# First expert layer: gated in place, context first, every third dot split between GpSimd and ScalarE

## The reference, cut to what matters

```python
def peer(h, w_q, sub_keys, u, v):          # h: (512, 1024); u, v: (16384, 1024)
    q = (h @ w_q).reshape(T, 8, 2, 128)
    s = einsum('thpd,hpnd->thpn', q, sub_keys)        # 8 heads x 2 sides x 128 keys
    sv, si = top_k(s, 16)
    cand = (sv[:, :, 0, :, None] + sv[:, :, 1, None, :]).reshape(T, 8, 256)
    fv, fi = top_k(cand, 16)
    idx = i1 * 128 + i2                               # 128 experts of each token
    g = softmax(fv)
    act = gelu(einsum('td,ted->te', h, u[idx]))
    return einsum('te,ted->td', g * act, v[idx])
```

## Time and profile before

| what | value |
|---|---|
| median of 3 runs | 3766.13 us (3762.77 to 3767.57) |
| profiled execution, its own time | 3757.47 us |
| its span | 3755.7 us |
| PE busy | 3287.2 us (88%) |
| DVE busy | 2497.0 us (66%) |
| ACT busy | 874.4 us (23%) |
| POOL busy | 883.1 us (24%) |
| DMA, mean | 262 GB/s |
| the stage `both_experts` in the span | 1475.8 to 2796.0 us |

### The profile page before, as it was taken

How to read it: one execution, slowest core, us unless ns; L and a number is a source line. 1 busy time by engine, 2 the same in 40 slices (tenths; PEclk the granted TensorE clock), 3 DMA queues, 4 the chain that set the end, 5 groups by cost and what they waited for, 6 DMA issues and landing times. The chain is left out here.

```text
span 3755.7 us, 56484 instructions
## 1 busy us (share of the span) xinstructions
PE 3287.2 (88%) x22342; PEld 2862.1 (76%) x22359; DVE 2497.0 (66%) x4759; ACT 874.4 (23%) x1601; POOL 883.1 (24%) x804
## 2 busy tenths in 40 slices
PE   9998999998999978999499987778879897599876
PEld 9976999986997657887388866666657687488875
DVE  5556656555664364589988857767775488877745
ACT  4345434334443353111022200000014411110000
POOL 0000000000000001014555545555530033423432
PEclk9999999999999999999799999999999999899998
DMA  7652666642662204279899999999971289999998
GB/s 245 224 176 101 234 222 205 230 160 90 230 211 84 73 1 152 73 234 394 306 355 369 363 364 403 400 403 404 404 290 49 97 336 409 349 361 342 406 409 316
DMA packets 298406, 983.68 MB, mean 262 GB/s; under 512 B 32928, under 2 KB 66720, under 8 KB 297248
## 3 DMA queue, kind: packets, MB, share of 16 engines
q1 hardware_dynamic: 187552, 577.36, 43.6%
q0 software_dynamic: 110592, 402.70, 27.6%
HBM read 960.01 MB, written 19.92 MB: 261 GB/s over the span
## 5 line engine op out<-in xcount | busy, mean ns | idle before, releaser
L325 PE MATMUL banks<-h_whole,ring 128*128 128x256 f32 (+1 forms) x4352 | 782.6, 336 | 138.0 <-ACT acts_out L2459 54.0
L325 PEld LDWEIGHTS banks<-h_whole,ring 128*128 128x128 f32 x4352 | 677.1, 193 | 214.4 <-ACT big L2914 84.7
L300 DVE TENSOR_TENSOR ring_lo<-ring,ring_hi 128x1024 fp32r<-128x1024 f32 x365 | 448.0, 1228 | 370.4 <-ACT ring_hi L294 351.1
L325 PE MATMUL banks<-scratch,ring 128*128 128x256 f32 x2048 | 490.1, 396 | 126.6 <-DVE scratch L2269 126.3
L325 PEld LDWEIGHTS banks<-scratch,ring 128*128 128x128 f32 x2048 | 392.8, 196 | 224.0 <-DVE scratch L2269 171.2
L294 ACT ACTIVATE ring_hi<-ring 128x1024 fp32r<-128x1024 f32 x365 | 386.7, 1059 | 571.1 <-PE banks L315 512.2
L325 PE MATMUL banks<-big,ring 128*128 128x128 f32 x2048 | 260.8, 281 | 50.7 <-DMA ring<-peer_v_dram 47.8
L311 PE MATMUL banks<-h_parts,ring_hi 128*128 128x256 f32 x1160 | 287.2, 286 | 6.0 <-PEq L664 3.4
L325 PEld LDWEIGHTS banks<-big,ring 128*128 128x128 f32 x2048 | 238.0, 192 | 70.2 <-DMA ring<-peer_v_dram 66.8
L312 PE MATMUL banks<-h_parts,ring_hi 128*128 128x256 f32 x1160 | 283.8, 282 | 0.0
L311 PEld LDWEIGHTS banks<-h_parts,ring_hi 128*128 128x128 f32 x1160 | 221.7, 191 | 18.3 <-issue 17.8
(11 more groups left out here) (366 smaller groups left out, 5852.5 us busy)
## 6 DMA issues: line engine op xcount, KB each, us to landing
ring<-peer_u_dram SPq DMA_DIRECT2D x256, 512.0 KB
ring<-peer_v_dram SPq DMA_DIRECT2D x256, 512.0 KB
big<-mod_w_dram SPq DMA_DIRECT2D x96, 512.0 KB, 4.6
ring<-ffn_gate_dram SPq DMA_DIRECT2D x88, 512.0 KB
ring<-ffn_up_dram SPq DMA_DIRECT2D x88, 512.0 KB
ring<-ffn_down_dram SPq DMA_DIRECT2D x88, 512.0 KB
ring<-peer_q_dram SPq DMA_DIRECT2D x32, 512.0 KB
act_store<-acts_out SPq DMA_DIRECT2D x128, 128.0 KB
```

The lines of the kernel that those rows point to most:

```text
L300: self.nc.vector.tensor_tensor(self.lo[:, self.slot(j)], self.ring[:, self.slot(j)], self.hi[:, n % 2].bitcast(F32), ALU.subtract).then_in ...
L325: ins = self.nc.tensor.matmul(out, self.ring[:, self.slot(j), c * P:(c + 1) * P], b, start=opens and m == 0, stop=opens and m == len(terms ...
```

## The change

- The stage before (`out_by_stream`) makes the ctx output first and norms it, so that `both_experts` begins with ctx tokens ready and norms x itself. Queries run as 32 tiles (16 for ctx, then the same 16 fetched again for x).
- Ctx is chosen first and by head pairs: for each pair of heads and token half a `level` (top 16 of four rows of 128) and a `choices` for two heads; 32 gathers become possible after each.
- Gelu writes into `A`, which stays in SBUF; `act_store`, its stores and loads, and the copy to `G` are gone. Gates are made for half of the keys at a time (128 steps, half of them woven into `fall`), and VectorE multiplies them from PSUM into `A`.
- Of the 256 dots every third (85) is taken from VectorE: GpSimd multiplies the row buffer by the tokens, in the POOL queue between the gathers, and ScalarE sums it with a copy that accumulates. ScalarE's place for each sum is planned from an estimated clock.
- Six row buffers instead of five; `spend` lets in a token step for every 2000 columns.
- The transposes of the choices stand behind `rise(95)` instead of `rise(57)`.

```diff
-ROWS = 5
+ROWS = 6
@@ both_experts
-    bufs = (whole_x[:, 0:D], whole_x[:, D:2 * D], whole_ctx[:, 0:D], whole_ctx[:, D:2 * D], spare[:, 0])
+    bufs = (whole_ctx[:, 0:D], whole_ctx[:, D:2 * D], k.rows[:, 0], whole_x[:, 0:D], whole_x[:, D:2 * D],
+            k.acts[:].rearrange("p r t -> p (r t)"))
+    LEAD = 4
+    order = [(0, t, 32 * b + p) for b in range(B) for t in range(NT) for p in range(32)] + [(1, 0, p) for p in range(LEAD)]
+    order += [(1, t, p + LEAD * (1 - t)) for p in range(P - LEAD) for t in (1, 0)] + [(1, 1, p) for p in range(P - LEAD, P)]
+    apart = [n for n in range(NT * P) if n % 3 == 2]
+    own_steps = [n for n in range(len(order)) if n not in apart]
+    EXP_X, SELECTED, FIRST_GATES = 93, 95, 96
+    steps_before, expected, QUERY, TILE = {}, {}, 3460, 3460
+    gates_after = [[n for n in range(STEPS) if FIRST_GATES + n * (N - 1 - FIRST_GATES) // STEPS == e] for e in range(N)]
+    gates_under = [[n for n in range(STEPS, 2 * STEPS) if (n - STEPS) * (HALF - 8) // STEPS == r] for r in range(N)]
...
-                sp.wait_ge(acted.sem, acted.after(e + 1))
-                sp.dma_start(k.act_store[e], k.acts[:, e % R]).then_inc(k.act_stored[e % R].sem, 16)
...
-                act_load(e, e - R + 1)
...
         @block.gpsimd
+            def multiply(n):
+                t = order[n][1]
+                pool.wait_ge(k.row_loaded[n % ROWS].sem, k.row_loaded[n % ROWS].after(16 * (n // ROWS + 1)))
+                nc.gpsimd.tensor_tensor(bufs[n % ROWS], bufs[n % ROWS], tok[:, t], ALU.mult).then_inc(multiplied.sem, 1)
+            for n, (table, t, p) in enumerate(order):
+                if not table and p % 32 == 0:
+                    pool.wait_ge(ready.sem, ready.after(n // 32 + 1))
+                before = n - ROWS
+                if before >= 0:
+                    freed = apart_used if before in apart else used
+                    pool.wait_ge(freed.sem, freed.after(nth[before] + 1))
                 nc.gpsimd.indirect_dma_start(bufs[n % ROWS], None, rows_of[table], ...)
+                if n - 2 in apart:
+                    multiply(n - 2)
@@ vector
-                    if spent >= 1150:
-                        spent -= 1150
+                    if spent >= 2000 and own_steps[step] < 32 * units:
+                        spent -= 2000
                         token_step()
+            for b in range(B):
+                for t in range(NT):
+                    level(1, t, b)
+                    LEVELS[1], steps_before["levels", 1] = count, step
+                    SETTLED[1] = choices(1, t, 2 * b, 2)
...
+            for n in range(2 * STEPS + 1):
+                if n < 2 * STEPS:
+                    mark(n)
+                if n:
+                    weigh(n - 1)
+                for _ in range(n % 2 if n < STEPS else 1 + (n % 3 == 0)):
+                    if n >= STEPS or step < OWN_DOTS:
+                        token_step()
+            while step < len(own_steps):
+                token_step()
@@ scalar
+            def apart_sums(last):
+                while summed_apart < len(apart) and apart[summed_apart] <= last:
+                    n = apart[summed_apart]
+                    summed_apart += 1
+                    act.wait_ge(multiplied.sem, multiplied.after(summed_apart))
+                    nc.scalar.activation(bufs[n % ROWS], bufs[n % ROWS], ACT.Copy,
+                                         accum_out=act_of[:, order[n][1], order[n][2]:order[n][2] + 1]).then_inc(apart_used.sem, 1)
+            def keep_up(now, coming):
+                ready_by = [n for n in apart if expected.get(n - 1, now) + 2000 < now]
+                within = own_steps[max(0, min([steps_before[w] for w in coming] + [len(own_steps)]) - 1)]
+                apart_sums(min(max(ready_by, default=0), within))
-                nc.scalar.activation(k.acts[:, e % R], k.ps[:, 4 + e % 2, 0:T], ACT.Gelu).then_inc(acted.sem, 1)
+                nc.scalar.activation(A[:, e], k.ps[:, 4 + e % 2, 0:T], ACT.Gelu).then_inc(acted.sem, 1)
```

More of the change, by code:

```diff
@@ L2197, in choices @@
+                pairings += 1
+                spend(wide)
+                made(nc.vector.tensor_copy(sif[m][:, rows], si[m][:, rows]), 32 * many)
+                dve.wait_ge(pairs.sem, pairs.after(pairings))
+                sixteen(range(many), cand, cand_left, fv[:, heads], fi[:, heads], lambda n: None)
                 dve.wait_ge(top.sem, top.after(count))
                 flat = fi[:, heads].rearrange("p a b -> p (a b)")
-                made(nc.vector.tensor_scalar(part[:, 0, cols], flat, 4, None, ALU.logical_shift_right), 128)
@@ L2216, in choices @@
-                if m == 1:
-                    dve.wait_ge(after.sem, after.after(n))
-                    nc.vector.scalar_tensor_tensor(idx[:, t], chosen[:, 0, cols], float(NKEYS), chosen[:, 1, cols], ALU.mult,
-                                                   ALU.add).then_inc(ready.sem, 1)
-                units += 1
-                return n
+                whole = made(nc.vector.tensor_copy(partf[:, :, cols], part[:, :, cols]), 32 * many)
+                picks = [pick[w][:, 0:16 * many] for w in range(2)]
@@ new lines, in choices @@
+                for w in range(2):
+                    dve.wait_ge(after.sem, after.after(at[w]))
+                    at[w] = made(nc.vector.reduce_sum(chosen[:, w, cols], picks[w], AX), wide)
+                if m == 1:
+                    dve.wait_ge(after.sem, after.after(at[1]))
+                    nc.vector.scalar_tensor_tensor(idx[:, t, 16 * first:16 * (first + many)], chosen[:, 0, cols], float(NKEYS),
+                                                   chosen[:, 1, cols], ALU.mult, ALU.add).then_inc(ready.sem, 1)
@@ L2378, in gates @@
                 last.then_inc(product.sem, 1)
             def fall(r):
-                pe.wait_ge(weighted.sem, weighted.after(r + 1))
-                k.whole(pe, Q + N + r, [(sums[:, c], c, hidden[:, r % R]) for c in range(KD)], False).then_inc(done.sem, 1)
+                k.whole(pe, V + r, [(sums[:, c], c, A[:, r]) for c in range(KD)], False).then_inc(done.sem, 1)
             for j in range(2):
-                query(j, 0)
+                query(j)
             sum_of_squares()
-            for j in range(2, R):
-                query(j, 0)
+            query(2)
@@ L2415, in _ @@
+                for n in gates_after[e]:
+                    gates(n)
             pe.wait_ge(kept.sem, kept.after(STEPS))
+            pe.wait_ge(acted.sem, acted.after(N))
             k.open_banks(range(4))
             for r in range(N - 1):
+                if r == HALF:
+                    pe.wait_ge(kept.sem, kept.after(2 * STEPS))
                 fall(r)
-            pe.wait_ge(weighted.sem, weighted.after(N))
+                for n in gates_under[r]:
+                    gates(n)
             for m in range(KD // 2):
-                k.whole(pe, Q + 2 * N - 1, [(sums[:, c], c, hidden[:, (N - 1) % R]) for c in (2 * m, 2 * m + 1)], False,
+                k.whole(pe, V + N - 1, [(sums[:, c], c, A[:, N - 1]) for c in (2 * m, 2 * m + 1)], False,
@@ L2950, in split_experts @@
     rstd_ends(k)
-    for b in range(ROWS):
-        k.row_loaded[b].ends(16 * len(range(b, len(order), ROWS)))
+    for b in range(W):
+        k.row_loaded[b].ends(16 * len(range(b, len(order), W)))
     tables.ends(16)
```

468 lines of the change are left out of this document (237 added, 231 removed).

## The result

The changed kernel takes 3993.14 us (median of 4 runs, 3987.88 to 3994.13); the kernel before took 3764.45 beside it (4 runs, 3754.14 to 3767.57). The ratio is 1.0614, 95% interval 1.0595 to 1.0633: 229 us slower. The forecast was 3739, its range 3665 to 3815.

The account below looks back on a forecast made before the run. The limit changes by stretch: TensorE, VectorE, both, then DMA at the end. Choosing to 2027, then 24, 173, 227, 310 and 8 us end the stage at 2769, 27 earlier: 3766 - 27 = 3739 us, range 3665 to 3815.

Parts of the forecast that it names:

- the overlap of TensorE's tiles with the choosing: In the choosing: TensorE reaches `rise(93)` by 1893 us, so its wait lies inside the choosing's end at 2027.
- First gather 1516, first dot 1522: Start of the choosing: first gather goes at about 1516 us instead of 1660.6, first dot at 1522.
- A round of 8.15 us: POOL queue in the choosing: product 2.5, issue 1.2, landing 4.1 and gaps 0.35 make 8.15 us per three gathers.
- The choosing ends at 2027: Choosing: 62 rounds of 8.15 us from 1522 end at 2027 us, against 1865.3 in the kernel before.
- First half of the gates 173: First gates after the choosing: VectorE's 142 us of steps and dots plus 31 us of blocking by GpSimd products.
- Second half 227: Gates under `fall`: VectorE 207 us and TensorE 205 us, with 10% added for mutual waits, give 227 us.
- The rest 310: End of the stage: 242 remaining pieces of gathers and tiles at 1.28 us each, DMA-bound, 310 us.
- The lock lengthens each round: Slower rival: dots hold the issue behind each product, round 9.05 us, 56 us on top, 3795 us; chance 0.30.
- The short chain: Faster rival: product 2.2, issue 0.94, landing 3.8, round 7.0 us, 71 us less, 3668 us; chance 0.16.
- Nothing: Rival: rounds of 8.5 to 8.7 us, earlier start and longer choosing cancel, 3759 to 3774 us; chance 0.12.
- The transfers were hidden anyway: Rival: the stage's end is not DMA-bound, so the 82 us of removed transfers are worth nothing; no separate chance given.
- VectorE's 2.4 us of spare time: In each round of the choosing VectorE has 2.4 us spare, nearly a whole product, so blocking is charged nothing there.

Follow-up runs that it names:

- e1_plan: Changed kernel without the cap on ScalarE's sums by later waits and without the demand for sums ahead of each move of scores: 3800.05 us.
- e2_cap: Changed kernel with only the cap on ScalarE's sums lifted, the demand ahead of x's scores kept: 3918.0 us.
- e9_due: Changed kernel with only the demand for sums ahead of x's scores removed, the sums still held behind later waits: 3889.81 us.
- e3_lag3: e1_plan with GpSimd multiplying each row three gathers after its issue instead of two: 3749.86 us.
- e6_sparse: e4_all_vector with a token step let in for every 2000 columns instead of 1350: 3733.64 us.
- e8_weave: e4_all_vector with two accumulating steps instead of one at another third of the 64 gate steps under `fall`: 3623.81 us.
- e12_beside: e7_five plus 85 extra GpSimd products of 1024 columns, one behind every third gather, into a buffer nothing reads: 3826.19 us.
- e4_all_vector: Changed kernel with all 256 dots on VectorE, none on GpSimd and ScalarE, a token step per 1350 columns: 3643.2 us.
- e7_five: e4_all_vector with five row buffers instead of six: 3656.59 us.
- e5_double: e3_lag3 with a second product in place behind each GpSimd product, waiting for it: 3983.63 us.

## Why the prediction was wrong

**The step that failed** is the overlap of TensorE's tiles with the choosing: "ScalarE follows a plan with a round of about 6.7 us, so at 8.15 it waits for products before its gelus, and TensorE follows it [...] so this wait is inside the 2027." The working took TensorE's tiles as free to stand at `rise(93)` by 1893 and let only the rounds set the end of the choosing. What the prediction read as a plan of times is an order. Sums up to row 98 stand in front of x's last queries, so tiles began at 1779 instead of 1605; and no later sum stands in front of gelu 70. Waits in both directions then follow one upon the other: rounds, with TensorE idle, then tiles, with the rounds stopped. Where the prediction has this wait inside the 2027, the trace has a hole of 235.8 us in the gathers and the last choice at 2240. Taking both conditions out brings 3993 to 3800 (e1_plan), and each alone leaves a hole (e2_cap, e9_due).

**Point by point.**
- First gather 1516, first dot 1522: 1510.2 and 1515.4. Right, and worth what was said.
- Product 2.5 us: 2.35. The Trainium skill's 2048-column figure in the GPSIMD Engine Reference, section 3.1, halved to 2.25 as an estimate, is nearer to this trace; the difference changes nothing.
- A round of 8.15 us: the 34th product starts at 1777.1 and the first at 1518.9, 258.2 / 33 = 7.82; from 2027.6 to the end of the choosing it is 8.2. The chain of row, product and issue is right, and e3_lag3 shows the landing in it.
- The choosing ends at 2027: 2240.2. That is 213 of the 257 us by which the stage ends later than forecast (3025.7 against 2769): 236 of the hole, less 7 for the earlier first dot and 16 for the rounds outside the hole.
- Choosing to gates 24: 21.7 (2240.2 to 2261.9). First half of the gates 173: 184 (2261.9 to 2446.1). Second half 227: 238 (to 2684). Terms of the right kind, 11 us short each.
- The rest 310: 335 (to 3019.3). The size of a piece was off. While TensorE's tiles and the gathers both fetch, the part runs near 400 GB/s as said, but TensorE is done early and waits 80.7 us for the last accumulating steps, and gathers alone need about 1.5 us each instead of 1.28. The order between tiles and gathers was missing from the sum.
- Outside the stage zero: 959.7 us behind it before and 960.4 after. Right.
- A tile of `rise`, 3.1: 3.45, the spacing of the gelus in the hole and in the trace of before too. By it `rise(93)` would have stood at 1926 instead of 1893, still inside the 2027.

The misses added up: 213 - 2 + 11 + 11 + 25 - 2 = 256.

**The rivals.** *The lock lengthens each round* was given 9.05 us, 3795 and a chance of 0.30. In the changed kernel the rounds stay below its bound of 8.7 (7.82 and 8.2). Its issues behind a product take a median of 0.98 us before the hole, but 1.78 after it, the 2.1 of the rival nearly. With the plan mended 44 of 61 take about 1.8, rounds are 8.75, and the kernel takes 3800. So the mechanism that the first rival named is real. It isn't the whole of the longer round: the issues have a mean of 1.57 us there, where the sum had 1.2, and from an issue's end to the next product it is 4.69, where the sum had 4.1 and gaps of 0.35. Why rows were used later was not followed up. The longer round puts the end of the choosing at 2057, 30 us after the forecast's 2027. The forecast of 3739 would have missed that kernel by 61 us, though its range would have held it. That the rival's 3795 is near 3800 is in part luck: its rounds of 9.05 are longer than measured, and the other 31 us come from behind the choosing. *The short chain* is out in all runs: the shortest rounds, 7.45 us with the product three behind (the 62 products of the choosing start from 1524.5 to 1979.0), are GpSimd's own work. *Nothing* did not come. *The transfers were hidden anyway* can't be read from these runs alone: no run puts the stores back. That the end is bound by what is left to fetch is shown by e6_sparse and e8_weave, which move pieces and pay or gain 1.5 and 0.9 us for each.

**Where the prediction charged nothing.** It let VectorE's 2.4 us of spare time in a round absorb each product. In a round that GpSimd paces that is nearly right. But it means that the edit had nothing to gain: a dot costs VectorE 1.14 us, and a product beside it 1.91 where VectorE is full (e12_beside), for a product of 1.90; the real one takes 2.35. From e4_all_vector to e3_lag3, 62 dots less and 62 products more should add 62 x (2.35 - 1.14) = 75 us to the choosing; it grows by 56 (1926.4 to 1982.3), with some hidden. Of the 107 us between the two runs 35 lie in the gates: the marks start from 1937.6 to 2343.0 in one and from 2000.3 to 2440.9 in the other. Where the last 16 lie was not followed up. The Trainium skill, SBUF — State Buffer, "SBUF: two separate sides", calls the shared ports of the two engines an exclusive lock. The traces agree for the dots: 1.91 us lost for 1.90 us of product. The estimate worked out from it in the prediction, that VectorE's round could grow to 8.2, was the better reason against the change.

What the change had right is visible once this part is out: the choosing by head pairs with the earlier gathers, activations gated in place and six buffers give 115 us, and 20 more with a better weave. The sixth buffer is 13 us of it (e7_five); how much each of the first two gives by itself was not tried, nor how much the later place of the transposes.

## What to carry to other kernels

An engine's program is an order, and a planned place is a wait with a due date: for each instruction put behind a condition, find what stands behind it on the same engine, and in a chain of three engines follow this once around. Before work is moved from VectorE to GpSimd, compare what GpSimd takes with what VectorE saves: elementwise work on one stopped elementwise work on the other here, so 2.35 us of product didn't pay for 1.14 us of dot. When a part is bound by what is left to fetch, count the pieces by kind, since those left alone at the end ran slower than a mixture.

## What the runs showed of the hardware

- A GpSimd product of 1024 columns took 2.35 us in place with two different inputs, and 1.90 with the same input twice and another output (which of the two counts was not tried). It took 3.22 where a held dot ran first (e5_double), and the issue of a gather took 1.78 instead of 0.94 to 0.98 in the same place (e1_plan).
- Beside a GpSimd product even a small VectorE operation can wait: a product of 128x32 elements took 2.33 us in the changed kernel, else 0.18. A dot could be held for the whole product:

```profile
1570.88 3.78 DVE L2139 CUSTOM_DVE_ANT_0 x_t<-x_t,h_whole 128x1024 f32<-128x1024 f32 x1
```

```profile
1571.22 2.35 POOL L2108 TENSOR_TENSOR acts_out<-acts_out,h_whole 128x1024 f32<-128x1024 f32 x1
```

- VectorE's searches, with one input, did not wait. In the changed kernel, inside the product that runs from 1518.95 to 1521.29, an index search takes the same 0.28 us as elsewhere, and the dot behind it is held:

```profile
1520.15 0.28 DVE L2185 FIND_INDEX8 big<-big 128x8 uint32<-128x128 f32 x1
1520.35 2.01 DVE L2139 CUSTOM_DVE_ANT_0 x_t<-x_t,h_whole 128x1024 f32<-128x1024 f32 x1
```

- A tile of `rise` takes 3.45 us (the spacing of the gelus at full clock in the hole), not the 3.1 used in the prediction.
- TensorE's granted clock is a mean of 0.68 of 2.4 GHz in the stretch where it waits in pieces of up to 47.9 us, between its levels of 1.2 and 2.4, and 1.00 in the stretch where it runs on.
